# Shared chunk products in the mLSTM scans, and the attention values scaled after their transpose

## The chip, the cores and the metric

The program runs on one core of a Trainium2 chip. The metric is the device time in microseconds of one execution. The profile is one execution; its engines are TensorE (PE, with its weight loads shown as PEld), VectorE (DVE), ScalarE (ACT), GpSimd (POOL) and SyncE (SP, which here only issues DMAs).

## The reference

One hybrid encoder layer over 1024 tokens of width 2048, float32 throughout. An RMS norm is followed by one input projection. Its columns feed two groups of heads, each group is gated by a SiLU path, and one output projection goes back into the residual.

- Eight attention heads of 128: q and k get an RMS norm and a partial rotation, three dilated windows are evaluated and mixed, and v is used as it comes from the projection. The projection is made from x before its norm, so each token's 1/rms of x still has to be applied to v.
- Four mLSTM heads (k and q of 128, v of 256). A forward and a backward scan go over the same tokens in chunks, with their own gates, and are summed. For one chunk:

```python
s = jnp.einsum('bhtd,bhsd->bhts', qc, kc) * w_intra
num = w_inter[..., None] * jnp.einsum('bhtd,bhde->bhte', qc, C) \
    + jnp.einsum('bhts,bhse->bhte', s, vc)
C_new = decay[..., None, None] * C + jnp.einsum('bhs,bhsd,bhse->bhde', wk, kc, vc)
```

The product of q and k of a chunk does not depend on the direction; the weights `w_intra`, `wk` and the state C do.

## The kernel before

The two projections are made as float32 products out of pairs of reduced-precision parts (a high part and a low remainder of each operand), with seven block products where eight would be usual. The program is a list of 560 units; from unit 14 on each unit is one such product on PE, 12 matmuls of 128x512 (lines 816, 818, 820), followed by whatever side work is written for that unit. Every engine walks the same list in its own order: ACT splits off the high part of the weights two units ahead (`w_hi`, line 1056), DVE the low part (`w_lo`, line 1340), and both take finished products out of PSUM (lines 1064 and 1069 on ACT, 1354 to 1373 on DVE). Products use PSUM banks 0 and 1 in turn; banks 2 to 7 belong to the side work. The order is written out by hand: a side job stands at a fixed offset from a starting unit, and an engine that waits in one job holds up all that stands behind it on that engine.

**mLSTM side work.** Head j starts at unit `M_START[j]` (line 62), one head after another. Chunks are of 128 tokens, so a head has 8 chunks and 16 steps: steps 0 to 7 go forward, steps 8 to 15 backward over the same chunks (`chunk_of`, line 140). Offsets below are from the head's start.

- Offsets 12 and 14 on PE: v is turned in `m_value_transposes` (line 879) into banks 2 and 3; DVE takes it out one unit later in `m_values` (line 1585), multiplied by a broadcast column from PSUM (line 1589).
- Every second unit from offset 20 on PE (`mlstm_pe`, line 935): first `step_products` (line 905) of the step before, then `step_inputs` (line 891) of this step. The products are three float32 matmuls of 257 columns, each in two instructions (lines 913, 916, 922; line 916 is left out at the first step of a direction). The inputs are k times q of the chunk (line 902, two instructions of 128x128, into bank 6) and the turned k (line 903, one instruction, into bank 7).
- One unit later on ACT (`m_step`, line 1151): an exponential makes the chunk's weights (line 1156), and a copy out of PSUM scales the turned k by a column (line 1161, 128x128).
- In the same unit on DVE: results of the step before (`m_results`, line 1617), then `m_mask` (line 1592) and `m_operands` (line 1603), whose last instruction multiplies k times q by the weights (line 1614).

The semaphore `m_x` tells of a step's inputs, `m_ops` of line 1614, `m_kw` of line 1161. At offset 57 the head's output is turned through banks 2 and 3.

**Attention side work.** Head h starts at unit `A_START[h]`, 357 + 17h (line 63). Offsets from there:

- 8 on SP: v of the head is loaded into `v_at`, transposed as the projection left it (features on partitions, tokens along the row).
- 10 on PE: the first of 8 `scores` (line 980); on DVE, `v_at` times the row of 1/rms of x (line 1769, in `attention_dve`, line 1761).
- 11 on PE: scores 1, then `value_transposes` (line 961), ten transposes into banks 2, 3 and 6; it waits for line 1769 by `a_vs`. On DVE: `masked` of scores 0 (line 1724, instructions of lines 1731 to 1738). On ACT: the exponential of scores 0 (line 1194).
- 12 on ACT: normalise 0, exponential 1, the weights' high part, then a copy of the first four turned blocks of v out of bank 2 (line 1225, in `attention_act`, line 1210). On DVE: reciprocal 0, mask 1, eviction, the weights' low part, then copies of the other four blocks (line 1794) and of the edge block (line 1797).
- 12 on PE: scores 2, then `prob_transposes` (line 996) of the first probabilities into banks 2 and 3 (lines 1005 to 1008); it waits for all copies of v (`a_va`, `a_vd`).

**SP.** `gate_stores` (line 495) issues a few DMAs of the norm and the gates at units 56 and 83. Behind them in the same queue stand the weights of the next group (line 447) and stores of products (lines 413 to 425). `mlstm_loads` (line 539) loads k and q of head j at offset 18, and from the second head on it waits for `m_x` of the head before.

Of the kernel before, what the change touches and what calls it, by code (L numbers as in the profile page):

```python
# [12 lines left out]
P = 128  # L13
# [135 lines left out]
def build_program(nc, xT, w_all, w_gates, vecs, norm_cols, m_cols, att_mask, rope, eye, tri, fin, y_dram, t_dram, ty_dram, eps_dram, rows_dram, rs_dram,  # L149
                  rot_dram, outT):  # L150
    with ExitStack() as ctx:
# [72 lines left out]
        vst = [view(6144, 1024), view(7168, 1024)]  # L224
        v1 = view(8192, TB * V1).rearrange("p (c e) -> p c e", e=V1)
# [77 lines left out]
        x_norm = sem("x_norm")  # L303
        g_act = sem("g_act")
# [49 lines left out]
        a_vs = sem("a_vs")  # L354
# [89 lines left out]
        def _(sp):  # L444
# [50 lines left out]
            def gate_stores(u):  # L495
                if u == 56:
                    sp.wait_ge(x_cols, 7)
                    sp.dma_start(eps_dram, spread1[0:2 * TB, 0, :]).then_inc(rows_out, 16)
                if u == 83:
# [39 lines left out]
            def mlstm_loads(j, at):  # L539
# [20 lines left out]
                if at == 18:  # L560
                    if j > 0:
                        sp.wait_ge(m_x, 16 * j)
                        sp.wait_ge(m_ops, 16 * j)
                    else:
                        sp.wait_ge(tl_done[1], t_made(1, 1))
# [221 lines left out]
        def _(pe):  # L787
# [103 lines left out]
            def step_inputs(j, n):  # L891
                c, d = chunk_of(n), n // TB
                cols = slice(c * P, (c + 1) * P)
                if n == 0:
                    pe.wait_ge(k_in, 16 * (j + 1))
                    pe.wait_ge(q_in, 16 * (j + 1))
                    if j == 0:
                        pe.wait_ge(g_dve, GD_COLS)
                if 16 * j + n > 0:
                    pe.wait_ge(m_ops, 16 * j + n)  # L900
                    pe.wait_ge(m_kw, 16 * j + n)
                nc.tensor.matmul(ps[:, 6, 2 * P:3 * P], kT[:, cols], qT[:, cols], start=True, stop=True)
                nc.tensor.transpose(ps[:, 7, 0:P], kT[:, cols], ident[:]).then_inc(m_x, 1)
# [31 lines left out]
            def mlstm_pe(j, at):  # L935
# [3 lines left out]
                if odd == 0:  # L939
                    if 1 <= n <= STEPS:  # L940
                        step_products(j, n - 1)
                    if 0 <= n < STEPS:
                        step_inputs(j, n)
# [17 lines left out]
            def value_transposes(h):  # L961
                pe.wait_ge(a_vs, h + 1)
# [33 lines left out]
            def prob_transposes(g, i):  # L996
                pe.wait_ge(a_p, 8 * g + i + 1)
                if i == 0:
                    pe.wait_ge(a_va, g + 1)
# [49 lines left out]
        def _(act):  # L1049
# [101 lines left out]
            def m_step(j, n):  # L1151
# [7 lines left out]
                act.wait_ge(m_x, 16 * j + n + 1)  # L1159
                end = 0 if d else P - 1  # L1160
                nc.scalar.activation(chunkbuf[:, i, 3, :], ps[:, 7, 0:P], ACT.Copy,
# [48 lines left out]
            def attention_act(h, at):  # L1210
# [10 lines left out]
                if at == 12:  # L1221
                    act.wait_ge(a_vtr, 3 * h + 1)
                    if h > 0:
                        act.wait_ge(a_pv, 4 * h)
                    nc.scalar.copy(vtok[:, 0:4, :], ps[:, 2, :].rearrange("p (b d) -> p b d", d=P)
                                   ).then_inc(a_va, 1)
# [101 lines left out]
        def _(dve):  # L1328
# [274 lines left out]
            def m_operands(j, n):  # L1603
# [8 lines left out]
                dve.wait_ge(m_x, 16 * j + n + 1)  # L1612
# [470 lines left out]
```

## Time and profile before

| | |
|---|---|
| three runs | 1993.58, 1998.57 and 1999.31 us, median 1998.57 |
| the profiled execution | 1991.36 us |
| its span, first to last instruction | 1989.6 us |
| granted TensorE clock, mean | 0.997 of full speed |
| matmuls, instructions | 9089 |

A line of the timeline gives an instruction's start and duration in us. PE's matmuls are pipelined: the next one starts before the one before it has ended, so what an instruction costs is the distance to the start of the next, not its duration. In brackets stands the time that an engine had been idle, and what ended the wait. SPq lines are DMA issues of the SyncE queue.

### The profile page before, as it was taken

How to read it: one execution, taken by the hardware profiler on the slowest of the kernel's cores; microseconds unless marked ns; L12 is line 12 of the kernel's file. 1: busy time of each engine (PE TensorE's matmuls, PEld its weight loads, DVE VectorE, ACT ScalarE, POOL GpSimd, SP SyncE). 2: the span in 40 equal slices, each digit the busy share in tenths (PEclk: the TensorE clock that was granted, in tenths of full speed). 3: DMA queues.
4: the chain of work that ended last, by engine and by line, in shares of the span. 5: the costliest groups of instructions: out<-in, count | busy, mean ns of one | idle time of the engine just before them, and what ended most of it. 6: DMA issues, size and time to landing. Idle time of an engine off the chain costs nothing.

```text
span 1989.6 us, 27114 instructions
## 1 busy us (share of the span) xinstructions
PE 1947.4 (98%) x9089; PEld 1589.4 (80%) x9089; DVE 1384.3 (70%) x2791; ACT 889.3 (45%) x1422; POOL 222.0 (11%) x240
## 2 busy tenths in 40 slices
PE   8999999999999999999999999999999899999999
PEld 6888887888888888888887878787787677777787
DVE  7677868678768768767767575665666857667655
ACT  6554335344335435334453335545446463455222
POOL 0241000110110010010000111110110111111111
PEclk9999999999999999999999999999999899999999
DMA  6676543564564465365369864462655836347554
GB/s 210 218 272 229 190 160 113 139 151 126 134 162 119 108 159 148 107 159 148 115 206 369 208 154 92 116 175 50 169 121 131 263 75 191 99 119 209 104 117 106
DMA packets 159337, 310.37 MB, mean 156 GB/s; under 512 B 17072, under 2 KB 36048, under 8 KB 155488
## 3 DMA queue, kind: packets, MB, share of 16 engines
q1 hardware_dynamic: 128432, 247.81, 37.8%
q0 software_dynamic: 28608, 53.49, 17.3%
q10 hardware_dynamic: 2160, 7.34, 1.0%
q8 instruction: 74, 1.21, 0.3%
q14 instruction: 63, 0.52, 0.1%
HBM read 198.60 MB, written 118.37 MB: 159 GB/s over the span
## 4 chain that ended last, share of the span: by engine, by line
PE 84%; DMA 5%; DVE 5%; issue 4%; ACT 1%; SPq 0%; POOL 0%; DVEq 0%; ACTq 0%; POOLq 0%
PE ps L816 22%; PE ps L820 21%; PE ps L818 21%; PE ps L1019 3%; PE ps L988 2%; PE ps L1005 2%; DMA arena<-rot_dram 1%; PE ps L957 1%; PE ps L913 1%; PE ps L922 1%; PE ps L916 1%; PE ps L1023 1%; DMA rot_dram<-arena 1%; ACT w_hi L1056 1%; PE ps L1021 1%
## 5 line engine op out<-in xcount | busy, mean ns | idle before, releaser
L816 PE MATMUL ps<-t_hi,w_hi 128*128 128x512 f32 x2184 | 872.0, 399 | 24.4 <-issue 9.7
L820 PE MATMUL ps<-t_hi,w_lo 128*128 128x512 f32 x2184 | 853.5, 391 | 0.0
L818 PE MATMUL ps<-t_lo,w_hi 128*128 128x512 f32 x2184 | 853.2, 391 | 0.0
L816 PEld LDWEIGHTS ps<-t_hi,w_hi 128*128 128x128 f32 x2184 | 411.5, 188 | 125.3 <-issue 45.9
L820 PEld LDWEIGHTS ps<-t_hi,w_lo 128*128 128x128 f32 x2184 | 411.2, 188 | 87.7
L818 PEld LDWEIGHTS ps<-t_lo,w_hi 128*128 128x128 f32 x2184 | 412.1, 189 | 79.6
L1340 DVE TENSOR_TENSOR w_lo<-s_tmp,w_hi 128x512 fp32r<-128x512 f32 x312 | 221.5, 710 | 180.0 <-ACT w_hi L1056 169.2
L1056 ACT CAST w_hi<-s_tmp 128x512 fp32r<-128x512 f32 x312 | 193.9, 622 | 292.7 <-PE ps L820 273.2
L1340 DVE TENSOR_TENSOR w_lo<-w_raw,w_hi 128x512 fp32r<-128x512 f32 x234 | 165.4, 707 | 146.9 <-ACT w_hi L1056 140.6
L1056 ACT CAST w_hi<-w_raw 128x512 fp32r<-128x512 f32 x234 | 145.4, 621 | 225.4 <-PE ps L820 225.3
L413 POOL DMA_DIRECT2D fin_dram<-xt x32 | 28.1, 878 | 850.8 <-ACT xt L1069 829.7
L1064 ACT COPY xt<-ps 128x512 f32<-128x512 f32 x78 | 45.8, 587 | 110.5 <-PE ps L820 110.4
L1200 ACT ACTIVATE arena<-arena,sums 128x704 f32<-128x704 f32 x64 | 56.4, 882 | 79.0 <-DVE sums L1744 79.0
L1069 ACT COPY xt<-ps 128x512 f32<-128x512 f32 x78 | 45.6, 585 | 98.6 <-PE ps L820 98.3
L1370 DVE TENSOR_TENSOR xt<-ps,xt 128x512 f32<-128x512 f32 x78 | 53.8, 689 | 47.4 <-PE ps L820 46.7
L1156 ACT ACTIVATE arena<-arena,g_cols 128x128 f32<-128x128 f32 x64 | 25.9, 405 | 132.1 <-DVE arena L1601 132.1
L1194 ACT ACTIVATE arena<-arena,mins 128x704 f32<-128x704 f32 x64 | 56.7, 887 | 49.1 <-DVE mins L1738 49.0
L1354 DVE TENSOR_TENSOR xt<-ps,xt 128x512 f32<-128x512 f32 x78 | 53.6, 688 | 26.2 <-PE ps L820 25.6
L1373 DVE TENSOR_TENSOR xt<-ps,xt 128x512 f32<-128x512 f32 x78 | 53.7, 688 | 23.6 <-PE ps L820 23.5
L988 PE MATMUL ps<-arena 128*128 128x512 f32 x128 | 65.9, 596 | 3.4 <-DVE arena L1721 2.2
L1364 DVE TENSOR_TENSOR xt<-ps,xt 128x512 f32<-128x512 f32 x78 | 53.6, 688 | 17.2 <-PE ps L820 16.6
L1750 DVE COPY arena<-ps 128x256 f32<-128x256 f32 x64 | 27.0, 422 | 51.9 <-PE ps L1023 33.1
(225 smaller groups left out, 2390.5 us busy)
## 6 DMA issues: line engine op xcount, KB each, us to landing
w_raw<-w_all_dram SPq DMA_DIRECT2D x320, 256.0 KB, 4.0
fin_dram<-xt SPq DMA_DIRECT2D x128, 256.0 KB, 4.3
fin_dram<-xt POOLq DMA_DIRECT2D x128, 256.0 KB, 5.0
arena<-fin_dram SPq DMA_DIRECT2D x64, 512.0 KB, 7.3
outT_dram<-xt POOLq DMA_DIRECT2D x60, 256.0 KB, 4.1
arena<-xT_dram SPq DMA_DIRECT2D x44, 256.0 KB, 6.0
arena<-xT_dram SPq DMA_DIRECT2D x16, 512.0 KB, 4.4
outT_dram<-xT_dram SPq DMA_DIRECT2D x16, 512.0 KB, 5.4
```

Of the source, the lines that this page charges most:

```text
L816: nc.tensor.matmul(ps[:, bank, :], hi, t_hi[:, n, k, :], start=new and k == 0, stop=False, skip_group_check=True)
L818: nc.tensor.matmul(ps[:, bank, :], hi, t_lo[:, n, k, :], start=False, stop=False, skip_group_check=True)
L820: mm = nc.tensor.matmul(ps[:, bank, :], lo, t_hi[:, n, k, :], start=False, stop=k == KP - 1, skip_group_check=True)
L988: nc.tensor.matmul(ps[:, 4, :], q, by_class(a_k)[:, :, h * P:(h + 1) * P], start=True, stop=True)
L1019: nc.tensor.matmul(out, vtok[:, 4 * h + b, :], pT[:, b, :], start=b == 0, stop=False)
L1056: nc.scalar.copy(w_hi[:, b % 3, :], src).then_inc(hi_done, 1)
L1194: nc.scalar.activation(prob[:, i % 2, 0:KEYS], prob[:, i % 2, 0:KEYS], ACT.Exp, bias=mins[:, i % 2:i % 2 + 1], scale=-1.0, accum_out=sums[ ...
L1200: nc.scalar.activation(prob[:, i % 2, 0:KEYS], prob[:, i % 2, 0:KEYS], ACT.Copy, scale=sums[:, 2 + i % 2:3 + i % 2]).then_inc(a_p, 1)
L1340: nc.vector.tensor_tensor(w_lo[:, b % 3, :], src, w_hi[:, b % 3, :].bitcast(F32), ALU.subtract).then_inc(lo_done, 1)
L1354: nc.vector.tensor_tensor(x2, bank, x1, ALU.add).then_inc(ev_d, 1)
L1370: nc.vector.tensor_tensor(x1, bank, x1, ALU.add).then_inc(ev_d, 1)
L1373: nc.vector.tensor_tensor(x2, bank, x2, ALU.add).then_inc(ev_d, 1)
```

## The change

In the mLSTM, k times q and the turned k of a chunk are made at the forward step only, for all eight chunks into places of their own: k times q in banks 6 and 7, the turned k in banks 2 and 3. The backward steps read them there. The first chunk now also waits until DVE has taken the turned v out of banks 2 and 3. In the attention, v is turned unscaled, and the 1/rms is applied when v leaves PSUM: ACT's one copy becomes four scaled copies of 128x128, DVE's two copies become multiplications by a broadcast column, and DVE's multiplication of `v_at` goes. The columns come from the row of 1/rms through a scratch row in DRAM: one store at unit 58 and four small loads at unit 100 on SP's queue, into `xq` and part of `epsx`, which are free by then.

```diff
+        v_cols, edge_cols = xq, epsx[0:CLASSES * EDGE, 0, 0:2]
...
+                if u == 58:
+                    sp.wait_ge(x_norm, 1)
+                    sp.dma_start(xrs_dram, xrs[0:1, :]).then_inc(xrs_out, 16)
+                if u == 100:
+                    sp.wait_ge(xrs_out, 16)
+                    sp.wait_ge(x_cols, 7)
+                    sp.wait_ge(x_rms, 1)
+                    sp.wait_ge(x_pe, 2)
+                    for half in range(2):
+                        sp.dma_start(v_cols[:, 4 * half:4 * half + 4],
+                                     xrs_dram[0, half * HALF:(half + 1) * HALF].rearrange("(n r) -> n r", r=CLASSES)
+                                     ).then_inc(v_cols_in, 16)
+                        lo = HALF if half == 0 else HALF - CLASSES * EDGE
+                        sp.dma_start(edge_cols[:, half:half + 1], xrs_dram[0, lo:lo + CLASSES * EDGE].unsqueeze(1)
+                                     ).then_inc(v_cols_in, 16)
...
-                        sp.wait_ge(m_x, 16 * j)
+                        sp.wait_ge(m_x, 8 * j)
...
-            def step_inputs(j, n):
-                c, d = chunk_of(n), n // TB
+            def chunk_inputs(j, c):
+
                 cols = slice(c * P, (c + 1) * P)
-                if n == 0:
+                if c == 0:
                     pe.wait_ge(k_in, 16 * (j + 1))
                     pe.wait_ge(q_in, 16 * (j + 1))
+                    pe.wait_ge(m_v, 2 * j + 2)
                     if j == 0:
                         pe.wait_ge(g_dve, GD_COLS)
-                if 16 * j + n > 0:
-                    pe.wait_ge(m_ops, 16 * j + n)
-                    pe.wait_ge(m_kw, 16 * j + n)
-                nc.tensor.matmul(ps[:, 6, 2 * P:3 * P], kT[:, cols], qT[:, cols], start=True, stop=True)
-                nc.tensor.transpose(ps[:, 7, 0:P], kT[:, cols], ident[:]).then_inc(m_x, 1)
+                if 16 * j + c > 0:
+                    pe.wait_ge(m_ops, 16 * j + c)
+                    pe.wait_ge(m_kw, 16 * j + c)
+                nc.tensor.matmul(flat(6)[:, cols], kT[:, cols], qT[:, cols], start=True, stop=True)
+                nc.tensor.transpose(flat(2)[:, cols], kT[:, cols], ident[:]).then_inc(m_x, 1)
...
                     if 1 <= n <= STEPS:
                         step_products(j, n - 1)
-                    if 0 <= n < STEPS:
-                        step_inputs(j, n)
+                    if 0 <= n < TB:
+                        chunk_inputs(j, n)
...
             def value_transposes(h):
-                pe.wait_ge(a_vs, h + 1)
+                pe.wait_ge(v_raw, 16 * (h + 1))
...
-                    pe.wait_ge(a_va, g + 1)
+                    pe.wait_ge(a_va, 4 * g + 4)
                     pe.wait_ge(a_vd, 2 * g + 2)
...
-                act.wait_ge(m_x, 16 * j + n + 1)
+                act.wait_ge(m_x, 8 * j + c + 1)
                 end = 0 if d else P - 1
-                nc.scalar.activation(chunkbuf[:, i, 3, :], ps[:, 7, 0:P], ACT.Copy,
+                nc.scalar.activation(chunkbuf[:, i, 3, :], flat(2)[:, c * P:(c + 1) * P], ACT.Copy,
...
-                    nc.scalar.copy(vtok[:, 0:4, :], ps[:, 2, :].rearrange("p (b d) -> p b d", d=P)
-                                   ).then_inc(a_va, 1)
+                    act.wait_ge(v_cols_in, 64)
+                    for b in range(4):
+                        nc.scalar.activation(vtok[:, b, :], ps[:, 2, b * P:(b + 1) * P], ACT.Copy, scale=v_cols[:, b:b + 1]
+                                             ).then_inc(a_va, 1)
...
-                dve.wait_ge(m_x, 16 * j + n + 1)
+                dve.wait_ge(m_x, 8 * j + c + 1)
                 dve.wait_ge(m_w, 16 * j + n + 1)
-                nc.vector.tensor_tensor(chunkbuf[:, i, 1, :], ps[:, 6, 2 * P:3 * P], chunkbuf[:, i, 0, :], ALU.mult
+                nc.vector.tensor_tensor(chunkbuf[:, i, 1, :], flat(6)[:, c * P:(c + 1) * P], chunkbuf[:, i, 0, :], ALU.mult
...
-                if at == 10:
-                    dve.wait_ge(v_raw, 16 * (h + 1))
-                    nc.vector.tensor_tensor(v_at, v_at, xrs[:], ALU.mult).then_inc(a_vs, 1)
...
-                    nc.vector.tensor_copy(vtok[:, 4:8, :], ps[:, 3, :].rearrange("p (b d) -> p b d", d=P)
-                                          ).then_inc(a_vd, 1)
+                    dve.wait_ge(v_cols_in, 64)
+                    nc.vector.tensor_tensor(vtok[:, 4:8, :], ps[:, 3, :].rearrange("p (b d) -> p b d", d=P),
+                                            v_cols[:, 4:8].unsqueeze(2).to_broadcast([P, 4, P]), ALU.mult).then_inc(a_vd, 1)
                     dve.wait_ge(a_vtr, 3 * h + 3)
-                    nc.vector.tensor_copy(vedge[0:CLASSES * EDGE],
-                                          ps[0:CLASSES * EDGE, 6, 0:256].rearrange("p (h d) -> p h d", d=P)
-                                          ).then_inc(a_vd, 1)
+                    nc.vector.tensor_tensor(vedge[0:CLASSES * EDGE],
+                                            ps[0:CLASSES * EDGE, 6, 0:256].rearrange("p (h d) -> p h d", d=P),
+                                            edge_cols.unsqueeze(2).to_broadcast([CLASSES * EDGE, 2, P]), ALU.mult
+                                            ).then_inc(a_vd, 1)
```

## Rows read from the trace of the kernel before

**Rows 1.** The page: busy time of each engine, and the chain that ended last.

```profile
PE 1947.4 (98%) x9089; PEld 1589.4 (80%) x9089; DVE 1384.3 (70%) x2791; ACT 889.3 (45%) x1422; POOL 222.0 (11%) x240
PE 84%; DMA 5%; DVE 5%; issue 4%; ACT 1%; SPq 0%; POOL 0%; DVEq 0%; ACTq 0%; POOLq 0%
```

**Rows 2.** Groups by line, PE: count | busy us, mean ns of one | idle before.

```profile
L902 PE MATMUL ps<-arena 128*128 128x128 f32 x128 | 24.6, 273 | 0.0
L903 PE MATMUL ps<-ident,arena 128*128 128x128 f32 x64 | 17.4, 273 | 0.0
```

**Rows 3.** Timeline, PE, a backward step with products and inputs: start, duration.

```profile
482.14 0.59 PE L913 MATMUL ps<-arena 128*128 128x257 f32 x2
...
483.44 0.38 PE L902 MATMUL ps<-arena 128*128 128x128 f32 x2
483.66 0.27 PE L903 MATMUL ps<-ident,arena 128*128 128x128 f32 x1
483.69 0.48 PE L816 MATMUL ps<-t_hi,w_hi 128*128 128x512 f32 x1
484.01 0.39 PE L818 MATMUL ps<-t_lo,w_hi 128*128 128x512 f32 x1
```

**Rows 4.** Timeline, PE, the products of the last step, with no inputs behind them.

```profile
517.65 0.59 PE L913 MATMUL ps<-arena 128*128 128x257 f32 x2
...
518.76 0.59 PE L816 MATMUL ps<-t_hi,w_hi 128*128 128x512 f32 x1
519.19 0.39 PE L818 MATMUL ps<-t_lo,w_hi 128*128 128x512 f32 x1
```

**Rows 5.** Timeline, DVE and PE, the step of head 0 with the least room.

```profile
472.91 0.29 DVE L1614 TENSOR_TENSOR arena<-ps,arena 128x128 f32<-128x128 f32 x1 [0.27 <-ACT arena L1156]
475.05 0.59 PE L913 MATMUL ps<-arena 128*128 128x257 f32 x2
```

**Rows 6.** Waits of PE in the attention, 1130 to 1800 us: total us, times, longest.

```profile
PE ps L1005 <- DVE arena L1797: 2.5, 6, 0.6
...
PE ps L988 <- DVE mins L1738: 1.0, 1, 1.0
```

**Rows 7.** Timeline, DVE, ACT and PE, attention head 0, offsets 10 and 12.

```profile
1174.41 1.22 DVE L1769 TENSOR_TENSOR arena<-arena,xrs 128x1024 f32<-128x1024 f32 x1
...
1183.02 0.69 DVE L1340 TENSOR_TENSOR w_lo<-w_raw,w_hi 128x512 fp32r<-128x512 f32 x1 [1.02 <-ACT w_hi L1056]
...
1184.23 0.41 DVE L1797 COPY arena<-ps 64x256 f32<-64x256 f32 x1
...
1182.82 0.58 ACT L1225 COPY arena<-ps 128x512 f32<-128x512 f32 x1
...
1184.78 0.63 PE L1005 MATMUL ps<-ident,arena 128*128 128x128 f32 x4 [0.55 <-DVE arena L1797]
```

**Rows 8.** Timeline, DVE and PE, attention head 5, offsets 10 and 11.

```profile
1587.41 1.24 DVE L1769 TENSOR_TENSOR arena<-arena,xrs 128x1024 f32<-128x1024 f32 x1
1588.55 2.31 DVE L1834 TENSOR_TENSOR t_lo<-t_lo,t_hi 128x2048 fp32r<-128x2048 f32 x1
...
1591.20 0.40 PE L820 MATMUL ps<-t_hi,w_lo 128*128 128x512 f32 x1
1592.59 1.12 PE L988 MATMUL ps<-arena 128*128 128x512 f32 x2 [1.00 <-DVE mins L1738]
```

**Rows 9.** Groups by line, ACT and DVE, instructions like the new ones.

```profile
L1161 ACT ACTIVATE arena<-ps,arena 128x128 f32<-128x128 f32 x64 | 23.6, 369 | 2.1
...
L1589 DVE TENSOR_TENSOR arena<-ps,rsrk 128x1024 f32<-128x1024 f32 x8 | 9.7, 1218 | 0.0
```

**Rows 10.** Timeline, DMA issues of SP around unit 100.

```profile
304.00 0.43 SPq L425 DMA_DIRECT2D fin_dram<-xt  x1
311.21 0.33 SPq L447 DMA_DIRECT2D w_raw<-w_all_dram  x1
```

**Rows 11.** Windows: busy us of PE, PEld, DVE, ACT and POOL, granted clock, DMA.

```profile
1587.00:1592.00 5.00, 4.58 (x12) 3.33 (x12) 5.00 (x7) 0.00 (x0) 0.00 (x0) 0.66 0.00 0
```

More of the change, by code:

```diff
@@ L146, in prepared_in, with build_program @@
     return u + 2 if u + 2 < UNITS else None
-def build_program(nc, xT, w_all, w_gates, vecs, norm_cols, m_cols, att_mask, rope, eye, tri, fin, y_dram, t_dram, ty_dram, eps_dram, rows_dram, rs_dram,
+def build_program(nc, xT, w_all, w_gates, vecs, norm_cols, m_cols, att_mask, rope, eye, tri, fin, xrs_dram, y_dram, t_dram, ty_dram, eps_dram, rows_dram, rs_dram,
                   rot_dram, outT):
@@ L303, in build_program @@
         x_norm = sem("x_norm")
+        xrs_out = sem("xrs_out")
+        v_cols_in = sem("v_cols_in")
         g_act = sem("g_act")
@@ L353, in build_program @@
         a_rope = sem("a_rope")
-        a_vs = sem("a_vs")
         a_zs = sem("a_zs")
@@ L2071 @@
     fin = nc.dram_tensor("fin_dram", (IN_TILES, 2, P, HALF), _mybir.dt.float32, kind="Internal").ap()
+    xrs_dram = nc.dram_tensor("xrs_dram", (1, SEQ), _mybir.dt.float32, kind="Internal").ap()
     y_dram = nc.dram_tensor("y_dram", (KT, P, SEQ), _mybir.dt.float32, kind="Internal").ap()
@@ L2079 @@
     outT = nc.dram_tensor("outT_dram", (O_TILES, P, SEQ), _mybir.dt.float32, kind="ExternalOutput").ap()
-    build_program(nc, *args, fin, y_dram, t_dram, ty_dram, eps_dram, rows_dram, rs_dram, rot_dram, outT)
+    build_program(nc, *args, fin, xrs_dram, y_dram, t_dram, ty_dram, eps_dram, rows_dram, rs_dram, rot_dram, outT)
     r = _run(nc, [arrays], core_ids=[0])
```

## The prediction

> **What bounds the kernel now.** I read the page first. PE is busy for 98% of the span, and the chain that ended last is PE for 84% [rows 1]. So PE sets the end, and an edit is worth time only where it takes work off PE's own stream or shortens one of the waits inside it. DVE and ACT have idle time on average, so work taken from or given to them counts only where PE stands waiting for it.
>
> The second view is the groups by line. The instructions that the change halves in number, k times q (line 902) and the turned k (line 903), are there 128 and 64 times at 273 ns each, and PE had no idle time before any of them [rows 2]. In the mLSTM stage PE never waits; its time there is the sum of what it is given.
>
> The third view is PE's timeline, which shows what such an instruction costs. Matmuls overlap: line 902's two start at 483.44 and line 903 starts at 483.66, 0.11 us per instruction, while each is shown as 0.27 long [rows 2, 3]. So I count by starts, never by busy time.
>
> The fourth is the list of PE's waits in the attention stage. The first turn of probabilities (line 1005) waited six times, 2.5 us in all, for DVE's copy of the edge block of v (line 1797), and once, for 1.0 us, the scores waited for DVE's masking [rows 6]. The change touches the queue in front of both.
>
> **The mLSTM part.** Removed are 8 of 16 steps' inputs in each of 4 heads: 32 times three PE instructions. With inputs, a step runs from 482.14 (line 913) to 484.01, the second matmul of the next product: 1.87 us [rows 3]. Without inputs, the last step of the same head runs from 517.65 to 519.19, the same second matmul: 1.54 us [rows 4]. The difference is 0.33 us, and 32 x 0.33 = 10.6 us. All of it lies on the path, since PE has no idle time there. Busy time would have said 3 x 0.273 x 32 = 26.2 us [rows 2], which is why I don't use it. The Trainium skill (TensorE: Matmul & The Clock Gate, section Back-to-back issue gap) gives about 81 ns per matmul of 128 columns in a sustained stream of weight loads and matmuls; an estimate from that page would be 96 x 0.081 = 7.8 us. The rows are of these very float32 instructions at 0.11 us, so they decide.
>
> Could the shorter steps meet a wait of another engine? PE's products of a step need DVE's line 1614. In the tightest step it ended at 473.20 (472.91 + 0.29), and PE came for it at 475.05: 1.85 us of room [rows 5]. A step loses 0.33, and two steps' losses together 0.66, so the room stays above 1 us. The waits on `m_x` that ACT and DVE lose in the backward steps bring nothing: line 1614 was held by ACT's exponential, not by PE [rows 5]. The PSUM places are others, the instructions are the same: no cost. The first chunk's new wait for DVE's second copy of v is for work written five units earlier (offset 15 against 20); I cost it at nothing, and were it late, the next product would stand behind it. SP's wait for `m_x` asks for an earlier signal than before.
>
> **The attention part, DVE.** Line 1769 goes, 8 times. From its start to the next start is 1.14 us (1587.41 to 1588.55) [rows 8], so everything behind it on DVE can be up to 1.14 us earlier, unless it waits for PE. What is late next is the chain of offsets 11 and 12: mask 0, ACT's exponential 0, the weights' split on ACT and DVE, reciprocal 0, mask 1, exponential 1, the next split (line 1340), the two copies of v. In head 0 the last copy ends at 1184.64 (1184.23 + 0.41), PE is released at 1184.78 after 0.55 us of idle time [rows 7]. Moved forward by 1.14, the copies end before PE comes in each of the six heads, whose longest wait is 0.6 [rows 6]; that leaves 0.5 us in hand for a mask that has to wait for its scores instead. The idle time understates the loss. It is counted from a matmul's shown end, 0.27 after its start, where the next could start 0.11 after [rows 2, 3]: 0.16 more each time. Gain: 2.5 + 6 x 0.16 = 3.5 us.
>
> The two copies become multiplications by a broadcast column out of PSUM, which the trace has as line 1589: 1.218 us for 1024 columns [rows 9], against 1.22 for line 1769 with both operands in SBUF [rows 7]. So form and place add nothing; for 512 columns and for the edge block I take the copies' own durations. The bounds are minus 0.1 (no row shows a multiplication beating a copy) and plus 0.2 us a head, inside the room.
>
> In head 5 DVE also rebuilds operands for the last projection. There the scores start at 1592.59 after masking, where PE could have gone on at 1591.43 (1591.20 plus one pitch of 0.23): 1.16 us, of which line 1769, further up in the same queue, is 1.14 [rows 8]. Gain: 1.1 us.
>
> **The attention part, ACT.** One copy of 0.58 us [rows 7] becomes four scaled copies of 128x128 out of PSUM; line 1161 is the same form, 0.369 us [rows 9]. At most that is 4 x 0.369 = 1.48 us end to end. In head 0 ACT's copy starts at 1182.82, DVE's split at 1183.02 and its last copy ends at 1184.64 [rows 7]; four scaled copies from 1182.82 would end at 1184.30, still 0.34 before DVE. Both move forward together, so ACT's 0.9 us more per head is hidden behind DVE's copies. If that cover went (DVE 0.4 faster, or ACT later), PE would wait for ACT, and behind the copies on ACT stands the normalising of the next probabilities. The Trainium skill (ScalarE: Activation LUTs, section What ACT_TABLE_LOAD costs) speaks against this edit: each ACTIVATE pays a fixed cost, and a per-partition scale adds about 93 ns, though neighbours overlap by as much. An estimate from that page is 4 x (186 + 93 + 107) - 3 x 93 = 1265 ns, inside the bound.
>
> **DMAs.** Five small ones are added on SP. An issue takes about 0.43 us [rows 10]. The four at unit 100 take 1.7 us and fall between the last issue of unit 98, done at 304.43, and the next at 311.21: 6.8 us with nothing to issue [rows 10]. Behind them stands a load of weights, which keeps its time. Their landing is not needed before the first attention head, over 800 us later. The store at unit 58 waits for a row that DVE makes at unit 54, ahead of what SP already waits for at unit 56.
>
> **Sum.** 10.6 + 3.5 + 1.1 = 15.2 us. The sum is made against the profiled execution, 1991.36 us (span 1989.6 and 1.8 around it), which would become 1976.2. That execution was 7.2 us quicker than the median of the three runs, 1998.57; taken from the median, the forecast is 1983.4 us.
>
> **The rivals.**
> - **PE waits for ACT instead of DVE.** The four copies, or something before them on ACT, end last, and the 3.5 us stay. Against it: 0.34 us of margin at the upper bound in head 0; for it: that margin is small. Gain 11.7 us, 1986.9.
> - **The backward steps have another limit.** If the chain from PE's products over DVE and ACT back to PE set the step, shortening PE's part would give nothing and only 4.6 us were left: 1994.0. Against it: no idle time and 1.85 us of room [rows 2, 5].
> - **Slower, through the four copies.** Their end would have to move so far that the new wait eats the other gains: 11.7 / 8 = 1.46 us a head past 1184.64 on the old scale, so 3.3 us for four copies, 0.82 each, over twice the row [rows 7, 9]. From there each long wait may also cost clock: after head 5's waits the granted clock averaged 0.66, a mix of 1.2 and 2.4 GHz, over 1587 to 1592 [rows 11], and the 12 matmuls of a product then took some 4.6 us by the same row, where 12 pitches of 0.23 are 2.7: 1.9 us lost. Eight such losses are 15 us: 2014.
> - **The change does not do what it says.** The diff makes inputs for 8 steps only, so I give this no share.
>
> **How the numbers follow.** The forecast has 0.72, PE waiting for ACT 0.18, another limit in the backward steps 0.06, slower 0.04. A difference under 0.3%, 6 us, can't be told from none. The first two cases are faster by more; I take 0.02 off for the scatter of runs: faster 0.88, same 0.08, slower 0.04. For the range, the low end is the fastest run, 1993.58, less 15.2, less two clock losses of 1.9 that may fall away when the waits shift: 1974.6. The high end is the first rival, 1986.9, plus 0.7 for the slowest run over the median, plus two clock losses: 1991.4.
>
> **What would show it.** Lines 902 and 903 with 64 and 32 instructions and still no idle time on PE in the mLSTM stage; a backward step 0.33 us shorter; no wait of line 1005 for line 1797, and none for the four copies; head 5's wait before its scores gone. A wait of line 1005 on ACT would say the first rival, idle time before line 913 the second. Clock losses in other places than before would make the sum wrong with all steps right.

## The result, and the profile after

The changed kernel takes 1984.67 us (median of 5 runs, 1981.98 to 1985.23), the kernel before 1995.75 (5 runs, 1993.58 to 1999.31): a ratio of 0.994, 95% interval 0.9927 to 0.9953, so 11.1 us less by the medians. The forecast was 1983.4, 15.2 us under the median it was taken from (1998.57, of three runs).

The profiled execution took 1985.23 us, its span is 1983.4. The page of the changed kernel, busy time and the chain that ended last (against [rows 1]):

```profile
PE 1939.9 (98%) x8993; PEld 1580.4 (80%) x8993; DVE 1375.3 (69%) x2783; ACT 891.3 (45%) x1446; POOL 221.9 (11%) x240
PE 86%; DMA 5%; DVE 4%; issue 3%; ACT 1%; SPq 1%; POOL 0%; DVEq 0%; ACTq 0%; POOLq 0%
```

PE has 96 instructions fewer, which is 32 steps of three, and DVE 8 fewer; ACT has 24 more. PE still sets the end.

PE's timeline of the changed kernel, the last step with inputs of a head (against [rows 3]) and the next one, which has none any more (line 932 is the first of the step's products, 921 and 922 are the chunk's inputs, 834 and 836 the first two matmuls of the next unit):

```profile
458.28 0.59 PE L932 MATMUL ps<-arena 128*128 128x257 f32 x2
...
459.57 0.38 PE L921 MATMUL ps<-arena 128*128 128x128 f32 x2
459.80 0.27 PE L922 MATMUL ps<-ident,arena 128*128 128x128 f32 x1
459.82 0.48 PE L834 MATMUL ps<-t_hi,w_hi 128*128 128x512 f32 x1
460.14 0.39 PE L836 MATMUL ps<-t_lo,w_hi 128*128 128x512 f32 x1
...
465.38 0.59 PE L932 MATMUL ps<-arena 128*128 128x257 f32 x2
...
466.49 0.58 PE L834 MATMUL ps<-t_hi,w_hi 128*128 128x512 f32 x1
466.91 0.39 PE L836 MATMUL ps<-t_lo,w_hi 128*128 128x512 f32 x1
```

With inputs it is 1.86 us from line 932 to line 836 (458.28 to 460.14), without them 1.53 (465.38 to 466.91): the 0.33 of the forecast, and no idle time in front of line 932.

PE's waits in the attention of the changed kernel, 1120 to 1800 us: total us, times, longest (against [rows 6]; lines 988 and 1005 are now 1007 and 1024):

```profile
PE ps L1007 <- DVE arena L1742: 1.9, 4, 1.0
...
PE ps L1024 <- DVE arena L1816: 0.2, 1, 0.2
```

The six waits of the turned probabilities for the edge block, 2.5 us, have become one of 0.2, and none is for ACT. The one left is head 2's. Head 5's wait for its mask is not in the list.

The timeline of the changed kernel at offset 12 of head 0, ACT, DVE and PE (against [rows 7]):

```profile
1176.82 1.14 ACT L1246 ACTIVATE arena<-ps,xq 128x128 f32<-128x128 f32 x4
...
1177.63 0.68 DVE L1813 TENSOR_TENSOR arena<-ps,xq 128x512 f32<-128x512 f32 x1
...
1178.23 0.41 DVE L1816 TENSOR_TENSOR arena<-ps,epsx 64x256 f32<-64x256 f32 x1
...
1178.99 0.40 PE L1011 MATMUL ps<-arena 128*128 128x128 f32 x2
1179.22 0.60 PE L1024 MATMUL ps<-ident,arena 128*128 128x128 f32 x4
```

ACT's four scaled copies take 1.14 us together and end at 1177.96; DVE's edge block ends at 1178.64, 0.68 later; PE is still at work on line 1011 then, and turns the probabilities from 1179.22 without waiting.

**One table for all profiles.** A single span scatters by more than the change is worth: two profiles of the kernel before have 1989.6 and 1999.9. Lengths of units do not. A unit is a product of twelve matmuls with what stands behind it, measured in PE's timeline from its first matmul to the next unit's first. "Backward" is offsets 36 to 54 of an mLSTM head (the four heads agree to 0.01), "offset 12" is summed over the eight attention heads, "waits for q" is what the stretch of offsets 20 to 36 is longer than 55.07, summed over the four mLSTM heads, so it holds the waits and what a fall of the clock behind them costs. The columns are in us, from one profile each; the time is the median, and the ratio is against the kernel before on the same chip.

| kernel | time | ratio (95%) | backward | offset 12 | head 5, offset 11 | waits for q |
|---|---|---|---|---|---|---|
| before | 1995.75 | 1 | 63.13 | 41.71 | 8.09 | 0.0 |
| after | 1984.67 | 0.9940 (0.9927 to 0.9953) | 60.45 | 38.31 | 7.09 | 1.9 |
| e1, mLSTM part alone | 1986.71 | 0.9943 (0.9926 to 0.9959) | 60.45 | 42.29 | 8.09 | 1.0 |
| e2, attention part alone | 1991.38 | 0.9967 (0.9953 to 0.9981) | 63.13 | 38.35 | 6.95 | 0.0 |
| e3, changed again | 1983.93 | 0.9928 (0.9904 to 0.9951) | 60.45 | 38.42 | 6.95 | 4.8 |
| e4, k and q at offset 17 | 1980.76 | 0.9914 (0.9897 to 0.9931) | 60.45 | 38.42 | 6.95 | 0.0 |
| e5, four copies three times | 1992.71 | 0.9976 (0.9964 to 0.9989) | 60.45 | 49.33 | 6.95 | 1.4 |
| e6, DVE's time put back | 1986.73 | 0.9944 (0.9925 to 0.9962) | 60.45 | 41.84 | 8.09 | 2.9 |
| e7, k times q each step | 1988.47 | 0.9966 (0.9951 to 0.9981) | 62.39 | 38.39 | 6.95 | 1.8 |
| e8, k and q at offset 19 | 1981.02 | 0.9915 (0.9892 to 0.9937) | 60.45 | 38.38 | 6.95 | 2.0 |
| e9, before again | 1996.77 | 1.0003 (0.9991 to 1.0015) | 63.13 | 42.25 | 10.29 | 0.4 |
| e10, offset 17 again | 1977.59 | 0.9901 (0.9882 to 0.9920) | 60.45 | 38.38 | 6.95 | 0.0 |
| e11, changed, third time | 1982.14 | 0.9922 (0.9902 to 0.9942) | 60.45 | 38.36 | 6.95 | 3.8 |
| e12, before, offset 17 | 1994.35 | 0.9991 (0.9977 to 1.0004) | 63.13 | 41.58 | 8.08 | 0.0 |

(In e9's 10.29 the scores start 5.58 us into the unit, as in the profile before; what follows takes 4.71 us in place of 2.51, at a granted clock of 0.56 from 1596 to 1602 us.) From before to after the three columns that were forecast give 4 x 2.68 + 3.4 + 1.0 = 15.1 us. The waits for q were not forecast. What the medians show less than that is looked for below. (One of the six runs of e11 took 6926.79 us, on its own; the median given is that of the other five.)

### The profile page after: what moved, and what is told of

It reads as the page before. It is cut to its first block, busy times and chain, and to the rows that moved or that the text cites. A ratio compares the mean times of both kernels' runs of the same rounds, so it can differ in the third digit from the quotient of the medians.

```text
span 1983.4 us, 26923 instructions
## 1 busy us (share of the span) xinstructions
PE 1939.9 (98%) x8993; PEld 1580.4 (80%) x8993; DVE 1375.3 (69%) x2783; ACT 891.3 (45%) x1446; POOL 221.9 (11%) x240
## 4 chain that ended last, share of the span: by engine, by line
PE 86%; DMA 5%; DVE 4%; issue 3%; ACT 1%; SPq 1%; POOL 0%; DVEq 0%; ACTq 0%; POOLq 0%
PE ps L834 22%; PE ps L838 22%; PE ps L836 22%; PE ps L1038 3%; PE ps L1007 3%; PE ps L1024 1%; PE ps L976 1%; PE ps L932 1%; PE ps L941 1%; PE ps L935 1%; DMA arena<-rot_dram 1%; PE ps L1042 1%; DMA rot_dram<-arena 1%; DMA arena<-rs_dram 1%; PE ps L853 1%
```

## The experiments

**The two parts apart (e1, e2), beside the whole (e3).** e1 puts the mLSTM lines of the diff alone on the kernel before, e2 the attention lines alone; e3 is the changed kernel. The core of each edit, with the rest left out: e1, and behind it e2:

```
-                    if 0 <= n < STEPS:
-                        step_inputs(j, n)
+                    if 0 <= n < TB:
+                        chunk_inputs(j, n)
```

```
-                    nc.vector.tensor_tensor(v_at, v_at, xrs[:], ALU.mult).then_inc(a_vs, 1)
...
-                    nc.scalar.copy(vtok[:, 0:4, :], ps[:, 2, :].rearrange("p (b d) -> p b d", d=P)
-                                   ).then_inc(a_va, 1)
+                    for b in range(4):
+                        nc.scalar.activation(vtok[:, b, :], ps[:, 2, b * P:(b + 1) * P], ACT.Copy, scale=v_cols[:, b:b + 1]
+                                             ).then_inc(a_va, 1)
```

> The mLSTM part alone on the kernel before; the attention is left as it was. Theory (each removed set of inputs is 0.33 us of PE's stream): the four backward halves are 10.6 us shorter together, the six waits before line 1005's successor in the attention stay at 2.5 us in all, the time is about 10.7 us below the kernel before. Rival (the backward steps are held by another engine): idle time of PE before the products of a step and a gain under 5 us. Beside it: if the wait for k and q before the first chunk (0.9 and 0.5 us in heads 0 and 2 of the changed kernel) comes from the change, it is here in the same two heads; if it is the scatter of the load's landing, it comes in other heads or not at all.

> The attention part alone on the kernel before (v scaled on its way out of PSUM, the five small DMAs); the mLSTM makes all 16 sets of inputs as before. Theory: the waits of the first probability transposes for the edge copy and head 5's wait for masking go, 4.6 us together, and the mLSTM steps keep their 7.10 us. Rival (the waits pass to ACT's four copies, or the 4.6 us are given back by the loads of head and tail): 1.5 us or less below the kernel before.

> The changed kernel once more. Its sum of parts was 15.2 us, its measured gain 11.1. Theory (the missing 4 us are scatter: waits for DMA landings, and stretches at half clock behind long waits, which fall otherwise in each execution): the same steps as in the first profile to 0.1 us in the mLSTM backward halves and at offset 12 of the attention heads, and other sizes of the waits before the first chunk, at units 111, 327, 449 and 509 and in the first 60 us. Rival (the change itself causes them): the same waits in the same places, 0.9 us in head 0, 0.5 us in head 2, 2.3 us at unit 327.

Measured: e1 10.6 us under the kernel before (1997.28 there, 1986.71 here), e2 5.9 (1991.38), e3 13.4 (1983.93). e1 has the short backward steps and the attention of before; e2 the long steps and the shorter offsets 12 and 11. The two kinds of gain do not touch each other: each is in its own column, at the same size with and without the other. By the columns e1 is 10.7 and e2 3.4 + 1.1 = 4.5, which lies within e2's interval (0.9953 to 0.9981 of 1997, 3.8 to 9.4 us). One number of e1's expectation missed: the six waits in its attention are 3.2 us and not 2.5, as head 2's unit at offset 12 is 5.9 long there (also in e9 and e12), where the profile before has 5.28. The other part of the expectations came out as scatter: the waits for q are in heads 0 and 2 of the profile after, in head 1 of e1, and in heads 0 and 1 of e3; unit 326 takes 5.16 us in the profile after, 3.84 in e3, and 5.11 in e9, which is the kernel before.

**What the backward step consists of (e7).** The product of k and q is made again in each backward step of the changed kernel, into the same place; the turned k is not.

```
+            def kq_again(j, n):
...
+                nc.tensor.matmul(flat(6)[:, cols], kT[:, cols], qT[:, cols], start=True, stop=True).then_inc(m_x, 1)
...
+                    elif 0 <= n < STEPS:
+                        kq_again(j, n)
```

> The changed kernel, with the product of k and q made again in each of the eight backward steps of a head, into the place where the forward step left it; the turned k is still made once. That is two of the three TensorE instructions that the change removes from a backward step. By the 0.33 us that the change won in each backward step for three instructions, at 0.11 us each, two of them cost 0.22 us in each of 32 steps: 7.0 us over the changed kernel, and a head's backward units (offsets 36 to 54) 62.2 us where the changed kernel has 60.45 and the kernel before 63.13. Rival A, the price follows the products and not their instructions, half for the product and half for the turned k: 0.165 in a step, 5.3 us, 61.8. Rival B, what was won is the wait for the semaphore ahead of the inputs and not the instructions: the whole 0.33 comes back, 10.7 us, 63.1.

The timeline of PE in e7, a backward step (line 939 is the first of its products, 929 the product made again):

```profile
463.23 0.59 PE L939 MATMUL ps<-arena 128*128 128x257 f32 x2
...
464.53 0.39 PE L929 MATMUL ps<-arena 128*128 128x128 f32 x2
464.67 0.47 PE L834 MATMUL ps<-t_hi,w_hi 128*128 128x512 f32 x1
464.98 0.39 PE L836 MATMUL ps<-t_lo,w_hi 128*128 128x512 f32 x1
```

The step is 1.75 us (463.23 to 464.98), between 1.53 and 1.86. The backward stretch is 62.39 us: 1.94 over the changed kernel in eight steps, 0.24 a step, 0.12 for each of the two instructions. The third, the turned k, is what is left to the kernel before, (63.13 - 62.39) / 8 = 0.09. So the theory's form holds, price by instruction, at 62.39 against its 62.2; half for the product (61.8) and a wait for the semaphore (63.1) are out.

**DVE's time put back (e6).** VectorE does an idle piece of work as long as line 1769 was (1.23 us each), where line 1769 stood, and TensorE's turning of v waits for it as it did for line 1769; v is scaled on its way out of PSUM as in the changed kernel. The lines for those waits are left out.

```
                 if at == 10:
+                    dve.wait_ge(v_raw, 16 * (h + 1))
+                    nc.vector.tensor_tensor(v_at, v_at, v_at, ALU.max).then_inc(a_vd, 1)
```

> The changed kernel, with VectorE's time at offset 10 of each head put back and nothing else: there VectorE takes the elementwise maximum of the loaded v tile with itself (the same values), TensorE's transposes of v wait for it as before, and v is still scaled on its way out of PSUM. If the attention part won by VectorE's 0.7 us of scaling taken out of the queue ahead of offset 12 and of the masking of head 5, both come back: waits of the probability transposes (L1024) on the edge copy of about 0.5 us in most heads, 3.4 us in all over the offsets 12, and 1.0 us of the scores (L1007) in head 5, so 4 to 5 us over the changed kernel, and the offset-12 units at 5.2 to 5.45 us again where the changed kernel has 4.72. Rival: the gain came by way of the DMA queues or of the place where the scaling is done; then the time stays within 1 us of the changed kernel and the offset-12 units at 4.7.

PE's waits in the attention of e6, 1120 to 1800 us:

```profile
PE ps L1024 <- DVE arena L1819: 2.7, 6, 0.6
...
PE ps L1007 <- DVE mins L1759: 1.0, 1, 1.0
```

Both waits of [rows 6] are back, six times and once, 2.7 and 1.0 us. By units it is 41.84 - 38.31 = 3.5 us at offset 12 and 8.09 - 6.95 = 1.1 in head 5: 4.6, as expected (the 0.7 us of scaling named there is 1.14 from start to start, [rows 8]). No wait of PE for the idle work itself is in the list. So the whole gain of the attention part is DVE's queue ahead of the masks and of offset 12, and neither the place of the scaling nor the transfers. (The median, 1986.73, is 2 to 6 us above those of the changed kernel, with intervals that overlap; the units decide.)

**The four copies three times (e5).**

```
-                    for b in range(4):
+                    for again in range(3):
+                        if again:
+                            act.wait_ge(a_va, 12 * h + 4 * again)
+                        for b in range(4):
...
-                    pe.wait_ge(a_va, 4 * g + 4)
+                    pe.wait_ge(a_va, 12 * g + 12)
```

> The changed kernel, with ScalarE's four scaled copies of v made three times over in each head (the same values to the same place), the probability transposes waiting for the last of the twelve. In the profile of the changed kernel the four copies of head 0 take 1.14 us from the first start to the last end (1176.82 to 1177.96 us) and TensorE came for them at 1179.22, unhindered. Theory: ScalarE has about 1.3 us to spare there, and a second and third round cost 1.14 us and some 0.1 to 0.2 us of semaphore each, 2.4 to 2.7 in all: the probability transposes (L1024) then wait for ScalarE by 1.1 to 1.4 us in each head, some 9 to 11 us over eight heads against the changed kernel. Rival A, the copies were already what TensorE waited for: 2.4 to 2.7 us in each head, 19 to 22 us. Rival B, ScalarE's lateness is paid by slack further on (its next activations or the exits of the products) and not at the transposes: under 3 us, with no wait of L1024 for ScalarE.

The timeline of e5 at the same place, head 0 (the two rows of PE are those that wait for ACT):

```profile
1172.99 2.98 ACT L1249 ACTIVATE arena<-ps,xq 128x128 f32<-128x128 f32 x10
...
1173.89 0.41 DVE L1819 TENSOR_TENSOR arena<-ps,epsx 64x256 f32<-64x256 f32 x1
...
1174.65 0.40 PE L1011 MATMUL ps<-arena 128*128 128x128 f32 x2
...
1176.07 0.63 PE L1024 MATMUL ps<-ident,arena 128*128 128x128 f32 x4 [1.02 <-issue]
```

ACT ends at 1175.97, DVE had ended at 1174.30; PE starts 0.10 after ACT. The list of waits shows it under two names:

```profile
PE ps L1024 <- issue: 6.9, 6, 1.5
...
PE ps L1024 <- ACT arena L1249: 3.1, 2, 1.6
```

Eight waits, 10.0 us; "issue" here is ACT as well, as the ends above show. Offset 12 is 49.33 us against 38.38 in e8, the sample of the changed kernel on the same chip, 11.0 more, and the time 11.7 us more by the medians. By units it is the theory's 9 to 11 and half of rival A's 19 to 22. So one round of copies was not what PE waited for. The twelve copies take 3.49 us from the first start (1172.48) to the last end, 2.35 more than four, and the units are 1.2 to 1.6 longer than in e8: ACT had 0.7 to 1.2 us in hand.

**The loads of k and q.** In the profile after, the first chunk's inputs waited in two mLSTM heads, and the list of waits names no engine for a cause. PE's waits from 380 to 970 us, the changed kernel:

```profile
PE ps L921 <- issue: 1.4, 2, 0.9
```

The same query on the changed kernel run again (e3):

```profile
PE ps L921 <- issue: 2.7, 2, 2.2
```

Line 921 needs q, and SP loads it at offset 18, two units of 2.72 us before its use. In the profile after it was issued at 399.34 and landed at 410.14, and PE went on at 410.23; in the one before it landed at 404.69, 1.5 us ahead of its use; in the other heads it was 0.4 to 1.7 us ahead. Four kernels were to move both loads: e4 and e10 have them one unit earlier (as below), e8 one later (19 in that line), and e12 is the kernel before with 17.

```
-                if at == 18:
+                if at == 17:
                     if j > 0:
```

> The changed kernel with k and q of a head loaded one unit earlier in SP's order. Theory (the loads land on the edge of when PE wants the first chunk, so PE's idle time there is the landing): q lands some 2 to 3 us before PE comes, no idle time before the first chunk in any head, 0 to 2 us below the changed kernel. Rival (the first chunk waits for something else, DVE's second copy of v or the gates): the idle time of up to 0.9 us stays.

> The changed kernel, with the loads of an mLSTM head's k and q issued one product unit later (offset 19, where the changed kernel has 18 and the faster version 17). A unit is 2.72 us there. In the profiles at offset 18 q landed 8.2 to 11.6 us after its issue and TensorE was kept waiting at the first chunk in 0 to 2 heads, by 0.5 to 2.2 us; at offset 17 it landed in 4.5 to 5.3 and nobody waited. Theory, the load at offset 18 stands at the edge, and each head that is late pays all of it: with the same 8.2 to 9.1 us to land, the first chunk waits for q in all four heads by 1 to 2.5 us, 4 to 10 us over the changed kernel, more where the landing is slower. Rival: the landing is set by what stands beside the load (the rows ahead of it in the queue, the pieces that are being stored), and past that crowd it lands in some 5 us: then the wait is under 0.5 us in most heads and the time within 2 us of the changed kernel.

e8 missed, and it is no test: SP issued the two loads no later than with offset 18 (q at 396.27 us, where e3 has 396.91 and the kernel before 396.37), behind the same two issues. SP had no other issue between the two offsets, so moving the block by one changed nothing. e8 is a fourth sample of the changed kernel. e4 does move the loads, ahead of a load of weights and of the row load.

SP's issues in the timeline of the changed kernel around the loads of the first mLSTM head (585 is k, 587 q, 567 the rows that are spread over all partitions):

```profile
397.93 0.33 SPq L450 DMA_DIRECT2D w_raw<-w_all_dram  x1
398.36 0.38 SPq L567 DMA_DIRECT2D arena<-rows_dram  x1
398.84 0.41 SPq L585 DMA_DIRECT2D arena<-fin_dram  x1
399.34 0.42 SPq L587 DMA_DIRECT2D arena<-fin_dram  x1
```

What the DMA engines did from there, 398 to 412 us, in 40 slices (busy tenths, and the rate):

```profile
DMA  0014699573557456769999999999999999999999
GB/s 0 0 64 64 222 322 196 31 26 16 20 25 37 18 79 155 180 193 298 347 375 351 354 331 287 304 315 189 209 193 195 228 195 167 152 173 189 225 293 316
```

The same of e10 (the earlier load, second time), SP from 391 us:

```profile
392.56 0.38 SPq L585 DMA_DIRECT2D arena<-fin_dram  x1
393.04 0.41 SPq L587 DMA_DIRECT2D arena<-fin_dram  x1
394.93 0.35 SPq L450 DMA_DIRECT2D w_raw<-w_all_dram  x1
395.37 0.39 SPq L567 DMA_DIRECT2D arena<-rows_dram  x1
```

And its DMA engines, 392 to 406 us:

```profile
DMA  0000177999999998755259999864200091989400
GB/s 0 0 0 0 12 164 269 433 380 386 433 375 415 398 375 228 69 29 16 29 120 148 189 195 205 171 135 94 41 6 0 0 94 23 176 164 205 76 12 0
```

In the changed kernel some 2.5 us (the seven slices from 31 to 18 GB/s) pass at 16 to 37 GB/s, after the row load has been issued and with the engines half busy; k and q stand behind it. In e10 they are first, and the engines move 375 to 433 GB/s for eight slices, until shortly before q lands at 397.65; the slow slices come afterwards, when the row load does. In e4 and e10 q lands in 4.4 to 6.6 us, and no head waits.

The row load is not the only neighbour. POOL issues the store of a finished product at 399.38 in the changed kernel, 0.04 us after q, and in e10 at 396.38, 3.3 us after q. The DMA engines of the changed kernel in the slow stretch, 400.4 to 402.9 us, and after it what the queues moved in the last 3.2 us before q landed, 407 to 410.2 (q0 is the queue of POOL's transfers):

```profile
DMA packets 111, 0.06 MB, mean 25 GB/s; under 512 B 2, under 2 KB 107, under 8 KB 111
```

```profile
q0 software_dynamic: 235, 0.43, 86.5%
q1 hardware_dynamic: 295, 0.22, 23.5%
```

In the first stretch almost nothing moves but pieces of 512 bytes, those of the row load; in the second the last of q comes in beside the store, which takes 86.5% of the engines. In the kernel before the store has 54.3% of the last 2.3 us. Offset 17 puts k and q ahead of the weights, the row load and the store together, and no run moves one of them alone.

> The kernel before, unchanged, so 1.000 of itself; its trace is wanted for the landing of q. In the nine profiles so far q, issued at offset 18 of an mLSTM head, landed 8.2 to 9.1 us after its issue in the eight heads of the two kernels with the mLSTM part of before, and over 9.1 us in 19 of the 28 heads of the seven with the changed mLSTM part (up to 11.6). Theory, the changed mLSTM part goes with a slower landing: here again 8.1 to 9.1 us in all four heads and no wait for q. Rival, it is scatter from execution to execution: one head at least over 9.2 us.

> The version with k and q loaded one unit earlier (offset 17), once more and beside the changed kernel on the same chip. At offset 17 the two loads leave before the last load of weights and the row loads of the forward head, and q landed in 4.5 to 5.3 us, 7 to 9 us ahead of its use. Theory: it saves the waits of the first chunks for q, 1 to 5 us in a profile of the changed kernel, about 2 in the middle, and nothing else: 2 us under the changed kernel here. Rival: the 3 us between the two in the first comparison were scatter, and the two are the same within 1 us.

> The changed kernel once more, beside the version with the earlier load. 10 to 14 us under the kernel before, as in the first two comparisons, with backward units of 60.45 us in each mLSTM head (offsets 36 to 54) and of 4.7 to 4.75 us at offset 12 of most attention heads. Theory of the slower landing: q takes over 9.1 us in two heads of four or more, with 1 to 5 us of waits at the first chunks. Rival, scatter: as in the kernel before beside it.

> The kernel before with the loads of k and q one unit earlier (offset 17 in place of 18) and nothing else. Theory: TensorE never waited for q in the kernel before, so nothing is saved: within 1 us of the kernel before, while the changed kernel wins about 2 us by the same edit. Rival: the earlier load helps by itself (it spreads the transfers around offset 18), 2 us or more here too.

The landing of q (line 569 before, 587 after), issue to landing in us, minimum, median and maximum over the four heads, first the kernel before again (e9), then the changed kernel (e11), then the earlier load (e10):

```profile
DMA to landing us min/median/max: 8.2/8.4/9.5
```

```profile
DMA to landing us min/median/max: 8.2/10.7/11.4
```

```profile
DMA to landing us min/median/max: 4.4/4.5/6.6
```

e9 falsified the theory in its strict form: one of its four heads took 9.46 us, and a unit longer by 0.4 came of it. The counts still differ: over 9.2 us in 1 of 12 heads with the mLSTM part of before (before, e2, e9) and in 20 of 32 with the changed one (after, e1, e3, e5 to e8, e11). These are three profiles against eight, so whether the change causes it is not shown; why a load that the change does not touch would land later stays open. The first mLSTM head, ahead of any step that the change shortens, has late landings as well.

By the medians e10 is 4.6 us under e11 and e4 3.2 under e3, more than the 2 us that were expected, with intervals that overlap. e12 is 2.1 under the kernel before, the size of its rival, but its interval reaches 1.0004; neither its profile nor the profile before has a wait for q from which the 2.1 could come. The time that the earlier load takes away is 1.9, 4.8, 2.0 and 3.8 us in the four profiles of the changed kernel with the load in its place; of the 4.8, the two waits listed are 2.7, and after the longer one the granted clock was 0.51 from 410 to 413.5 us. That is the size of what the medians lack against 15.2: 4.1, 1.8 and 0.9 us, while e8 lacks nothing. The changed kernel with k and q loaded one unit earlier has the two lowest ratios here, 0.9901 and 0.9914, but by time alone it is not told apart from e8 with 0.9915.

## Why the prediction was right, point by point

- **The mLSTM part** was forecast as 32 x 0.33 = 10.6 us and measured as 4 x 2.68 = 10.7, alone (e1) and in the whole. Counting by starts instead of busy time (26.2 us) made the difference. The Trainium skill (TensorE: Matmul & The Clock Gate, section Back-to-back issue gap) has some 81 ns for a matmul of 128 columns in a stream, by which the estimate was 7.8 us. The trace agrees for the turned k, at 0.09, and not for the product of k and q, whose two instructions cost 0.12 each (e7); [rows 3, 4] were the better guide.
- **The room of the shorter steps** was there: no wait before a step's products in any profile, so the rival of another limit (1994.0) is out.
- **Offset 12** was forecast as 3.5 us and measured as 41.71 - 38.31 = 3.4. The 0.16 that was added for each wait, for idle time that is counted from a shown end, was needed: five of the six units are shorter by 0.17 to 0.19 us more than their wait. The sixth, head 2's, kept 0.2 us of its wait, against the forecast that all six would go, and is only 0.13 shorter; that the sum still came out at 3.4 owes 0.14 to head 5, which had no wait there.
- **Head 5** was forecast as 1.1 and measured as 1.0 to 1.1. But "head 5's wait before its scores gone" was a poor sign. The wait is gone from the profile after and there again in e11:

```profile
1584.49 1.27 PE L1007 MATMUL ps<-arena 128*128 128x512 f32 x2
```

```profile
1585.70 1.12 PE L1007 MATMUL ps<-arena 128*128 128x512 f32 x2 [1.44 <-DVE mins L1759]
```

  Yet in both the scores start 4.44 us into their unit, against 5.58 before. The windows of the two show why (columns as in [rows 11]); first the changed kernel, then e11:

```profile
1580.00:1585.00 5.00, 4.80 (x13) 3.34 (x14) 4.96 (x10) 0.53 (x1) 0.00 (x0) 0.66 0.00 0
```

```profile
1581.00:1586.00 5.00, 3.30 (x13) 2.47 (x14) 4.96 (x11) 0.32 (x1) 0.00 (x0) 1.00 0.00 0
```

  DVE is busy all the time in both. In the first PE had a granted clock of 0.66 on average, a mix of 1.2 and 2.4 GHz, and its slower product filled the time; in the second it ran at 2.4 GHz, was through earlier and waited 1.44 us for the mask. When the scores start is DVE's matter, and DVE's 1.14 us is what was won. The fall of the clock cost nothing up to there, and 0.14 us in the scores behind it (7.09 against 6.95). The prediction priced such a fall at 1.9 us; by its own count by starts the product of [rows 11] took 4.4 us and not 4.6 (1587.02 to 1591.43), so 1.7, and where PE would have waited anyway even that is not lost. Only the range and the slower rival rest on this price.
- **ACT's four copies** were bounded at 1.48 us and took 1.14, starts 0.25 to 0.26 apart and 365 ns each; the cover was forecast as 0.34 us at that bound and is 0.68. The Trainium skill (ScalarE: Activation LUTs, section What ACT_TABLE_LOAD costs) gave an estimate of 1.27 us; the trace has less. The first rival (PE waits for ACT) and the slower one through the copies are excluded by the profile after, and e5 shows how far off they were: it takes two more rounds of copies, 2.35 us, for waits of 1.0 to 1.6 us a head. By the gain alone this could not be told: 11.1 us is nearer to that rival's 11.7 than to 15.2.
- **The scaled copies on DVE** cost what the copies did: 0.68 and 0.41 us before and after.
- **What failed** is the claim about PE in the mLSTM stage, "since PE has no idle time there": true of the profile before, and taken to hold after. The loads of k and q landed 0.4 to 1.7 us ahead of their use in it, and no term of the sum asked how much cover they had. In the four profiles of the changed kernel they took 1.9 to 4.8 us back. The new wait for DVE's copy of v, and the five small transfers, cost nothing that any profile shows.
- **The rest of the 15.2 against 11.1** looks like scatter. On the same chip the changed kernel was 11.1, 13.4 and 14.3 us faster by the medians, and e8, which issues the same in the same order, 15.8. In the pair of profiles, 6.1 us apart, 9.0 of the 15.1 are missing: the changed one began unit 14 3.0 us later (a start-up that the change does not touch), lost 1.9 with q, and the other 4.1 in units that vary from profile to profile, such as 326.
- **The time itself**, 1983.4 forecast and 1984.67 measured, is closer than the gain by luck: the median of three runs that it was taken from was 2.8 us above that of the five, 1995.75, and this made up for most of the 4.1 us that the gain was too high.

## What to carry to other kernels

Price a removed TensorE instruction by the distance of starts with and without it in the same stream, and a removed wait by the next thing on its queue. Then ask of every transfer beside it how long before its use it lands: a load that has only 1 to 2 us in hand can be the next wait, and moving it past slow neighbours took a single number here. Where one profile differs from the next by more than the change is worth, compare the lengths of units that repeat, which agree to 0.01 us, and read a wait that went away only together with the granted clock of its stretch.

## What was not expected of the hardware

- A load of 512 KB (q, over all profiles) takes 4.4 to 6.6 us from issue to landing ahead of a load of weights, a row load of 128 KB that is spread over all partitions, and a store by POOL. Behind the first two and beside the third it takes 8.0 to 11.6. In the slices after the row load's issue the engines are half busy at 16 to 37 GB/s, where the same engines move 375 to 433 on the big loads and a piece of weights.
- The same kernel's profiles differ by 10 us (1989.6 and 1999.9 for the kernel before), with mean granted clocks of 0.997 and 0.994 and waits of 1 to 3 us in other places; the backward stretches of the mLSTM heads, which have neither, are the same to 0.01.
- PE waiting on a semaphore of ACT is listed as "issue" in six of eight heads of e5 and as ACT in two, although ACT ended last in all eight.
